# Down projection of two feed-forward blocks: 20 of its 22 hidden tiles by a seven-product scheme in place of eight products

## What is computed

```python
# first block ("ffn"), followed by the gated embedding part ("ple")
h = rmsnorm(x, g_ffn[i])
gate = causal_dwconv3(h @ w_gate[i], ffn_conv_w[i], ffn_conv_b[i])
x = x + (jax.nn.silu(gate) * (h @ w_up[i])) @ w_down[i]
ple_gate = jax.nn.sigmoid(rmsnorm(x, g_ple[i]) @ w_ple_gate[i])
x = x + ple_gate * (p[i].astype(x.dtype) @ w_ple_proj[i])
# second block ("n2"), the last thing computed
x = x + (jax.nn.silu(h2 @ w_gate[l]) * (h2 @ w_up[l])) @ w_down[l]
```

## Time and profile before

| | before |
|---|---|
| median of 3 runs | 2559.43 us (2558.32 to 2561.62) |
| span of the profiled execution | 2557.0 us |
| what lies around the span, against that median | 2.4 us |
| PE busy | 2510.4 us, 98% |
| DVE / ACT / POOL busy | 1357.8 / 1054.9 / 1273.0 us |
| moved by DMA | 246.29 MB, mean 96 GB/s |
| down, first block | 934.8 to 1175.3 us |
| down, second block | 2314.0 to 2553.6 us |

### The profile page before, as it was taken

How to read it: one execution, slowest core, us unless ns; L and a number is a source line. 1 busy time by engine, 2 the same in 40 slices (tenths; PEclk the granted TensorE clock), 3 DMA queues, 4 the chain that set the end, 5 groups by cost and what they waited for, 6 DMA issues and landing times.

```text
span 2557.0 us, 34626 instructions
## 1 busy us (share of the span) xinstructions
PE 2510.4 (98%) x12210; PEld 2083.9 (81%) x12210; DVE 1357.8 (53%) x2481; ACT 1054.9 (41%) x1959; POOL 1273.0 (50%) x946
## 2 busy tenths in 40 slices
PE   8999999999999999999999999899999999999999
PEld 6888888888888888888877887689888888888887
DVE  5337775289666652225267888777156333333222
ACT  6346663253333332224256666576234333323120
POOL 2133324458666665444435554463356566657451
PEclk9999999999999999999999999999999999999999
DMA  4264314212222253211223222320422222226311
GB/s 158 75 193 125 112 62 169 95 54 96 83 91 76 81 211 127 83 60 51 90 76 94 63 63 75 107 68 18 157 75 83 75 91 83 80 102 231 107 50 67
DMA packets 99787, 246.29 MB, mean 96 GB/s; under 512 B 10624, under 2 KB 32416, under 8 KB 99360
## 3 DMA queue, kind: packets, MB, share of 16 engines
q1 hardware_dynamic: 99616, 244.08, 27.8%
HBM read 184.27 MB, written 55.05 MB: 94 GB/s over the span
## 4 chain that ended last, share of the span: by engine, by line
PE 92%; DVE 3%; POOL 2%; ACT 1%; issue 1%; DMA 1%; SPq 0%; ACTq 0%; DVEq 0%; POOLq 0%
PE PS L963 10%; PE PS L964 10%; PE PS L965 10%; PE PS L701 9%; PE PS L703 9%; PE PS L702 9%; PE PS L981 6%; PE PS L982 6%; PE PS L983 6%; PE PS L1233 2%; PE PS L835 1%; PE PS L806 1%; PE PS L933 1%; PE PS L935 1%; PE PS L934 1%
## 5 line engine op out<-in xcount | busy, mean ns | idle before, releaser
L701 PE MATMUL PS<-Hh,Wl 128*128 128x512 f32 x1072 | 433.4, 404 | 12.5 <-DVE Hl L1375 9.7
L703 PE MATMUL PS<-Hh,Wh 128*128 128x512 f32 x1072 | 420.2, 392 | 0.0
L702 PE MATMUL PS<-Hl,Wh 128*128 128x512 f32 x1072 | 419.6, 391 | 0.0
L3277 POOL TENSOR_TENSOR Wl<-Wr,Wh 128x512 fp32r<-128x512 f32 (+1 forms) x158 | 209.6, 1348 | 352.6 <-ACT Wh L2354 352.3
L3383 POOL TENSOR_TENSOR RG<-RW,RG 128x512 fp32r<-128x512 f32 x176 | 246.8, 1407 | 130.3 <-ACT RG L2682 130.3
L1832 DVE TENSOR_TENSOR XA<-PS,XA 128x512 f32<-128x512 f32 x192 | 132.5, 691 | 331.8 <-PE PS L983 331.8
L981 PE MATMUL PS<-Hh,RG 128*128 128x512 f32 x704 | 274.1, 389 | 0.9 <-POOL Hl L3479 0.5
L982 PE MATMUL PS<-Hl,RG 128*128 128x512 f32 x704 | 273.9, 389 | 0.0
L983 PE MATMUL PS<-Hh,RG 128*128 128x512 f32 x704 | 273.9, 389 | 0.0
L3383 POOL TENSOR_TENSOR RG<-SW,RG 128x512 fp32r<-128x512 f32 x120 | 165.2, 1377 | 171.4 <-ACT RG L2682 146.0
L965 PE MATMUL PS<-Hh,RG 128*128 128x512 f32 x640 | 249.0, 389 | 0.0
(11 more groups left out here) (366 smaller groups left out, 5144.0 us busy)
## 6 DMA issues: line engine op xcount, KB each, us to landing
RW<-in_wg SPq DMA_DIRECT2D x44, 512.0 KB, 3.6
RW<-in_wu SPq DMA_DIRECT2D x44, 512.0 KB, 4.5
R<-in_wd SPq DMA_DIRECT2D x88, 256.0 KB, 2.9
hgscr<-GB SPq DMA_DIRECT2D x44, 512.0 KB, 2.6
G<-hgscr SPq DMA_DIRECT2D x40, 512.0 KB, 6.6
Wr<-in_wi SPq DMA_DIRECT2D x27, 512.0 KB, 3.4
Wr<-in_wo SPq DMA_DIRECT2D x16, 512.0 KB, 3.3
spill<-X SPq DMA_DIRECT2D x16, 512.0 KB, 2.6
```

The source lines that it names most:

```text
L701: pe.matmul(ps(b), k.Wl[:, s, wc], xh[:, kx, sl], start=kk == 0, stop=False)
L702: pe.matmul(ps(b), k.Wh[:, s, wc], xl[:, kx, sl], start=False, stop=False)
L703: i = pe.matmul(ps(b), k.Wh[:, s, wc], xh[:, kx, sl], start=False, stop=kk == nk - 1)
L3277: i = pool.tensor_tensor(k.Wl[:, s, c], k.Wr[:, s, c], k.Wh[:, s, c].bitcast(F32), ALU.subtract)
```

## The change

- **Down.** Group 0 (hidden tiles 0 and 1) stays as it was: 16 tiles of 2 x 3 matmuls (`FIRST_DOWN`). The other 20 hidden tiles are 10 pairs. A step `x` (20 of them, 5 double pairs by 4 double rows `mp` of the output) takes a 2 by 2 block of `w_down` (two `m` by two `f`) against a 2 by 2 block of gated tiles (two `f` by two halves), for two pairs at once, in seven products p = 1, 6, 7, 5, 2, 4, 3, each 2 x 3 matmuls. Four of the seven weight operands are sums of blocks, made by DVE 256 wide (`down_sum`, into `R2` and `SX`); the other three are raw blocks. The seven pieces, 256 wide, are split by ACT and POOL, nine ahead, in a ring of twelve in `Wh`, `Wl`; those of the last two x go to free parts of `Hh`, `Hl`.
- **Combining.** Banks as in gate and up (two sets of four). Products 1 and 2 share a bank, 7 and 4, 5 and 3; the first of each is read out before the second is added on top, so PE waits for DVE's `dx` of 1, 7, 5 before it starts 2, 4, 3. Per x DVE reads seven products out (for x < 4 the first one is ACT's). What 1 and 6 give together stays in a kept buffer per `mp` and is added to three of the four output tiles once, in the last four x (one `fold` on DVE, two on POOL per x).
- **Gated operands.** Seven blocks of 512 per pair instead of four: b11, b21, b22 and four combinations. DVE makes these in `pair_first` and `pair_rest` while gate and up runs (four subtractions per pair), each block is stored by its own DMA of 256 KB (`part_store`), and whoever overwrites `GB` waits for those stores (`gb_free`). A pair is loaded back by three DMAs into the place of its low parts; ACT copies out the high parts (512 or 1536 wide), and the low parts are turned in place, blocks 0, 3, 6 by DVE (512 wide), 1 with 2 and 4 with 5 by POOL (1024 wide).
- **Around.** The last pieces of tile 21 run in the order 3, 4. `p`'s load and split, the squares and the scaled splits of "ple" move with the last three x and behind the loop; the last two rows are stored 7, 6.

```diff
+STEPS = (1, 6, 7, 5, 2, 4, 3)
+DOWN = [(x, p) for x in range(NX) for p in STEPS]
...
+        for m, half in FIRST_DOWN:
...
+            i.then_inc(*up(("full", b), "d0", tag, m, half))
+        for n, (x, p) in enumerate(DOWN):
+            b = BANK[x % 2][p]
+            begins = p in (1, 6, 7, 5)
+            if begins:
+                take(b)
+            if p in (2, 4, 3):
+                pe.wait_ge(*at("dx", tag, x, {2: 1, 4: 7, 3: 5}[p]))
+            pe.wait_ge(*at("w2_lo", tag, 8 + n))
+            for a, pair in enumerate(pairs_of(x)):
+                if x % 4 == 0:
+                    pe.wait_ge(*at("hg_lo", tag, pair, STEP[p]))
+                xh, xl = k.block(pair, STEP[p])
+                wh, wl = (w[:, 128 * a:128 * a + 128] for w in k.down_piece(tag, 8 + n))
...
+        def pair_rest(f):
+            _, b12, b21, b22 = k.pair_parts()
...
+            dve.tensor_tensor(b12, b22, b12, ALU.subtract).then_inc(*up("t", "ht", tag, f // 2, 2))
+            dve.wait_ge(*at("ht_out", tag, f // 2, 3))
+            dve.tensor_tensor(k.hd, b22, k.hd, ALU.subtract).then_inc(*up("t", "ht", tag, f // 2, 1))
+            dve.wait_ge(*at("ht_out", tag, f // 2, 4))
+            dve.wait_ge(*at("ht", tag, f // 2, 1))
+            dve.tensor_tensor(b21, b21, k.hd, ALU.subtract).then_inc(*up("t", "ht", tag, f // 2, 5))
...
+            if (m, half) == (0, 0):
+                for z in range(4):
+                    down_sum(tag, 0, z)
...
+            if (m, half) == (2, 1):
+                pair_rest(NF - 1)
+            if half and m in (4, 5):
+                down_sum(tag, 1, 2 * m - 8)
+                down_sum(tag, 1, 2 * m - 7)
+            if half and m in (3, 6):
+                hg_low(tag, m // 3, 0)
+                hg_low(tag, m // 3, 3)
...
+            if p == 7:
+                dve.wait_ge(*(at("xd0", tag, 2 * mp + 1, 1) if first else at("dx", tag, x - 4, 5)))
+                dve.tensor_tensor(x22, ps(b), x22, ALU.add).then_inc(*up("uv", "dx", tag, x, 7))
...
+            if 0 < i < 5 and x + 2 < NX:
+                down_sum(tag, x + 2, i - 1)
+            if i == 5 and x // 4 < 4:
+                for pair, j in hg_due(x, (0, 3, 6)):
+                    hg_low(tag, pair, j)
...
+            if x // 4 < 4 and i == 4:
+                for pair, j in hg_due(x, (1, 4)):
+                    hg_low(tag, pair, j)
+            if x >= NX - 4 and i in (2, 3):
+                z, p2 = (("21", 4), ("12", 3))[i - 2]
+                out = k.XA[:, 2 * mp + 1, h0] if i == 2 else k.XA[:, 2 * mp, h1]
...
+                pool.tensor_tensor(out, out, k.kept(mp), ALU.add).then_inc(*up("fold_g", "fold", tag, x, z))
```

637 lines of the change are left out of this document (431 added, 206 removed).

## The result

The changed kernel takes 2544.18 us (median of 4, 2539.95 to 2546.39) against 2559.71 us in the same rounds (4, 2558.32 to 2561.62): a ratio of 0.9938, 95% interval 0.9923 to 0.9952. It is faster, by 15.5 us where 37.4 were forecast. Its profiled execution has a span of 2540.7 us, 16.3 us under that of before.

What follows compares the result with a forecast made beforehand. PE was taken as the bound, busy 98% of the span. 2557.0 - 54.4 + 6 (middles) + 7.5 (starts) + 3.5 (first down's end) = 2519.6 us; with 2.4 between span and median, 2522 us, range 2504 to 2546.

Steps and rivals of the forecast that it cites:

- What can be won: Both downs: 240 fewer matmuls at 0.2267 us each, 54.4 us at most.
- The middle: Middle of down: DVE's waits for POOL cost PE 0.2 us per x while x < 16, 3 us per block.
- break-even of 0.54: Middle of down: wait in us per two-SBUF-operand DVE instruction, 5.5 per x, that uses up DVE's 2.97 us room.
- The rival that shared access sets the pace: Middle of down: POOL's and DVE's two-operand instructions never overlap, 23 or 28 us; 2539 to 2544 us, chance 0.22.
- the slower one: Rival, middle of down: nearly every such instruction waits 1.08 us, 95 us lost; 2611 us, chance 0.07.
- The start: Where down begins: PE waits for DVE's late queue, 5 us in the first block, 2.5 in the second; ends 0 and 8.
- Near the 20th us: Start of down: the last two rows of `spill` land when they are read out, hidden but without room.
- Behind the first down: First down's end: POOL's late last fold delays read-out, low parts and squares before PE's first statistics; 3.5 us, 0 to 9.
- Gate and up: Gate and up: 40 added DVE subtractions per block and smaller stores cost 0, with 3 us as the far end.
- The order of tile 21: Gate and up's end: products in order 3, 4 are the same work, 0 us.

Runs made afterwards that it cites:

- e7b: Changed kernel with one extra 256-wide DVE sum per x, for x from 2 to 15 in down: 2545.6 us, one run.
- e8b: Changed kernel with POOL writing zeros instead of 256-wide low parts in down, from the twelfth piece on: 2541.7 us, one run.
- e4: Changed kernel with x = 0's sums one behind each of the first four read-outs, x = 1's behind the last low parts: 2547.9 us, ratio 0.9955.
- e3: Changed kernel with the last two x's POOL folds and the last x's four additions of squares given to DVE: 2541.2 us, ratio 0.9928.
- e19: As e17, plus POOL waiting for the first block's last convolution step before group 0's two low parts: 2540.0 us, ratio 0.9925.
- e13: Changed kernel with the four subtractions per pair left out in both blocks, stores kept: 2531.1 us, one run.
- e9: Changed kernel with tile 21's products back in the order 4, 3: 2540.4 us, ratio 0.9929.
- e5: Changed kernel with the last two of an odd tile's three subtractions, and their stores, four pieces later: 2544.9 us, ratio 0.9945.
- e16: Changed kernel with the pair subtractions and their stores in gate and up two pieces later: 2542.4 us, ratio 0.9936.
- e14: Changed kernel with gate and up's pair subtractions made by POOL instead of DVE: 2544.0 us, ratio 0.9940.
- e1: Changed kernel with the four subtractions per pair done on one column of 512 only: 2537.6 us, ratio 0.9916.
- e17: Changed kernel with group 0's low parts moved back three pieces and down's first eight weight parts also later: 2543.3 us, ratio 0.9936.
- e11: Changed kernel, first down's end: last two x's folds on DVE, PE's statistics, first root and p's split later: 2537.6 us, ratio 0.9915.

## Why the prediction was right or wrong

- **What can be won**: right, 54.4 us forecast, 55.3 from the starts of the matmuls; the 240 matmuls are gone from the counts at an unchanged pace.
- **The middle, 3 us per block**: the mechanism right, the size too high, 0.6 and 0.3 us. DVE was busy 142.92 of 156 us, 8.72 us per x of 9.52. By the prediction's own sum, 6.55 + 5.5 w = 8.72, the wait w is 0.39 us, under the break-even of 0.54. I had taken "a value about there"; the rows that I had, 0.19 and 0.70 us, have 0.45 as their middle, and that would have given no wait. POOL waits too: it is busy 141.29 of 156 us, 8.6 us per x where the prediction had 7.5. e7b shows how near it was. The rival that shared access sets the pace (28 us) fell, and with it the slower one, which needed 0.79 us. Waits as long as it feared do exist, beside the 1024-wide instructions (L2048 in e8b, 2.31 us beside one of 2.40), but they are few per x. The Trainium skill, page "SBUF — State Buffer", section "Who interferes with whom", says that a VectorE instruction with two SBUF inputs contends with a GpSimd one that reads SBUF and not with one that only writes it; e8b agrees, 0.41 us beside memsets.
- **The start, 5 and 2.5 us**: the size near, 6.4 and 4.4 measured, and DVE's queue the cause, but the place wrong. The prediction had 3 us of waiting behind the four sums ahead of the first read-out, in the first 8 us; there PE waited 0.67 us, and in the second block not at all. Most of it, 2.35 + 1.61 us, came 17 and 22 us in, behind the subtractions, to which it gave no wait of their own, and behind low parts. e4 shows it: without the sums in front nothing was won. That the total came out near is partly luck. "Near the 20th us" for the last rows of `spill` was wrong too: they landed some 27 us in, issued at 969.68. DVE, late itself, waited only 0.47 us for them in after, but 3.86 in e4.
- **Behind the first down, 3.5 us, at most 9**: wrong in size, 13.7. The wait that it described, POOL's last fold, read-out, low parts and squares ahead of the first statistics, was right: 3.40 us. What it left out is the reverse, that the second weights stand behind a fold and a sum of squares, so PE waits for them as well, 5.1 us with the short wait for the first ones (e3: gone when POOL has neither). And it had no term for the clock: behind each of the two long waits nine matmuls in a row start over 3.55 us instead of 1.81, 3.5 us in all, and the eight of L803 take 1.84 us for 0.95. Together 5.1 + 3.4 + 3.5 + 0.9 = 12.9 of the 13.7.
- **Gate and up, 0, at most 3**: the step that failed most, 12.0 us in the first block. I divided the added DVE time by the 350 us of the stretch, found 305 of 350 busy (296.57 measured) and took no wait at all. The losses are at two places. From 600 to 640 us DVE had been busy 37.8 of 40 us even before, with PE never waiting, a row that a stretch of 350 us hides; before, then after:

```profile
600.00:640.00 40.00, 40.00 (x178) 33.09 (x177) 37.77 (x38) 14.77 (x26) 33.23 (x23) 1.00 0.29 105
```

```profile
600.00:640.00 40.00, 36.41 (x152) 29.30 (x151) 36.95 (x36) 12.24 (x22) 30.15 (x21) 0.96 0.37 134
```

  In after PE and DVE both wait in this stretch. Three subtractions of 1.6 to 1.8 us beside POOL's low parts, with a 1.91 us wait for POOL's product at their head, put DVE's queue behind, and PE then waited 3.5 us for it. From 920 to 946 us the cause is not the subtractions alone: the prediction did not speak of POOL's order in gate and up at all, and the low parts of group 0 had moved three pieces forward, into the convolution's last products (e19, which parts them: 5.1 us less than after). Without the subtractions (e13) this place loses less, 2.1 us of waiting: the low parts start at 915.75 and 919.71 there and are through before the products at 922.43. Waits are 0.41 + 3.53 + 4.29 = 8.2 us of the 12.0. The rest is the clock: behind 627.99 and 938.98 us matmuls are 0.43 us apart again, with 152 matmuls in the 40 us from 600 and 87 in the 26 from 920, where 176 and 115 fit, 5.5 + 6.3 us lost with the waits. The order of tile 21, "the same work, 0", cost 1.2 us in the second block (e9): product 3 right behind 5 needs 5's read-out at once, where PE waited 0.8 us.
- **The sum.** Terms 6 + 7.5 + 3.5 + 0 = 17 forecast, 0.9 + 10.8 + 13.7 + 13.2 = 38.6 measured. So the forecast failed by two terms, gate and up at nothing (13.2) and the end of the first down at 3.5 (13.7), and by pricing every wait at its length alone. The rival with the nearest time, 2539 to 2544 us, was right by accident: its 28 us in the middle of down were not there.

What stays open: how the 3.53 us wait at 627 us can be removed. Neither another place (e5, e16) nor another engine (e14) did it, only less work (in e1 it is 1.8 us, in e13 gone). No kernel that keeps the subtractions but spares the convolution was tried. At the start of down the loads of the residual's last rows were never moved alone.

## What to carry to other kernels

Where a bound engine is fed by two others, price a change at the joints, not over the stage: take the busy share of the feeding engines in stretches of 20 to 40 us around every hand-over, and list what the change moves past each queue on both, as well as what it adds. A long instruction on POOL next to a DVE queue that PE waits for can cost most of its length (in e17 two convolution products took 4.0 us more beside two low parts of 5.32 together); part them with a wait or give them another place, and see whether the next joint takes the gain back. And a wait of 2 us or more on PE can be dearer than its length, since the matmuls behind it may run at the lower clock level, here for about 2 us more.

## What was not expected of the hardware

- After the waits of 3.3 to 5.3 us in after, e3, e9 and e11 PE's matmuls start 0.43 us apart for some 3 to 5 us (clock 0.50, 1.2 GHz), in e9_order only from the fourth one behind its 3.62 us wait at 938.14. In e13_no_pair a wait of 2.07 us at 930.54 was followed by the same (0.50 from 932 to 934 us), while the 2.35 us at 963.03 in after left the clock at 1.00.
- A one-column DVE instruction with two SBUF inputs takes 0.54 to 0.72 us on average beside POOL's work, 0.15 us at the shortest (e1_tiny_pair), a 256-wide one beside memsets 0.41 us (e8b_pool_memset).
- DVE's TENSOR_SCALAR in fp32 (L1830), with one SBUF tile as input, takes 0.55 us while POOL is idle (944.17 in after) and 1.09 us on average in the first block's gate and up of after, so it seems to wait as well.
